# Channel products of the Fourier branch folded into the last attention pair, pair order, norm products and output weights moved, in an eight-core encoder layer

## The reference

```python
proj = x @ w_in                       # q, k, v (24 heads of 64), u_f (512), gate_a, gate_f (1024 each)
# three groups of 8 heads: windows 128, 512, 2048 with dilations 1, 4, 16; relative-position bias
attn = sum over groups of softmax(lse)[g] * out[g]         # 512 wide
y_attn = attn @ w_attn_out
f = real(fft2(u_f as (positions, 4 groups of 128 channels), ortho))
y_four = f @ w_fourier_out
mix = (sigmoid(gate_a) * y_attn + sigmoid(gate_f) * y_four) @ w_out
h = layer_norm(alpha * x + mix)
out = layer_norm(alpha * h + square(relu(h @ w_up + b_up)) @ w_down + b_down)
```

## Time and profile before

| | |
|---|---|
| median of 3 runs | 2229.06 us (2223.16 to 2231.4) |
| the profiled execution | 2229.99 us, span 2228.5 us on core 4 |
| spans of the 8 cores | 2204.2 to 2228.5 us |
| mean granted clock of TensorE, core 4 | 0.981 |
| PE busy | 2072.9 us (93%) |
| DVE busy | 1087.7 us (49%) |
| ACT busy | 694.3 us (31%) |
| POOL busy | 178.6 us (8%) |

### The profile page before, as it was taken

How to read it: one execution, slowest core, us unless ns; L and a number is a source line. 1 busy time by engine, 2 the same in 40 slices (tenths; PEclk the granted TensorE clock), 3 DMA queues, 4 the chain that set the end, 5 groups by cost and what they waited for, 6 DMA issues and landing times.

```text
span 2228.5 us, 39457 instructions; the slowest of 8 cores (2204.2 to 2228.5 us)
## 1 busy us (share of the span) xinstructions
PE 2072.9 (93%) x10660; PEld 991.5 (44%) x10866; DVE 1087.7 (49%) x1704; ACT 694.3 (31%) x1182; POOL 178.6 (8%) x234
## 2 busy tenths in 40 slices
PE   5999778899989999999999999989999999999997
PEld 2454334444444444444444544443444444444443
DVE  1235567534574555555232366675337535554543
ACT  1446445222232221313124455532221413122130
POOL 1000000000000110202020000000000002020011
PEclk9999999999999999999999999989999999999999
DMA  9428456554143453548731123154113345454352
GB/s 143 68 39 107 88 86 126 121 156 86 38 171 133 154 192 132 195 134 216 190 96 34 25 46 60 27 125 161 29 20 123 134 136 188 151 179 171 122 200 95
DMA packets 61468, 261.56 MB, mean 117 GB/s; under 512 B 8050, under 2 KB 19314, under 8 KB 41084
## 3 DMA queue, kind: packets, MB, share of 16 engines
q1 hardware_dynamic: 34084, 194.54, 25.8%
q0 software_dynamic: 27168, 64.49, 18.6%
HBM read 306.43 MB, written 35.91 MB: 154 GB/s over the span
## 4 chain that ended last, share of the span: by engine, by line
PE 81%; DMA 9%; DVE 5%; issue 3%; ACT 1%; POOL 0%; DVEq 0%; POOLq 0%; ACTq 0%; SPq 0%
PE bank L329 76%; PE bank L327 4%; DMA pool<-wup_s 3%; DMA pool<-rden_s 2%; DMA pool<-xt 1%; DMA pool<-wdn_s 1%; ACT pool L318 1%; DMA pool<-dft 1%; PE bank L984 1%; DVE pool L1158 1%; DVE pool L704 0%; DVE pool L922 0%; DVE pool L709 0%; DVE pool L655 0%; DMA rden_s<-pool 0%
## 5 line engine op out<-in xcount | busy, mean ns | idle before, releaser
L329 PE MATMUL bank<-pool 128*128 128x512 bf16 (+2 forms) x8686 | 1957.5, 379 | 76.4 <-DMA pool<-xt 22.6
L329 PEld LDWEIGHTS bank<-pool 128*128 128x128 bf16 x8892 | 870.2, 100 | 1053.4 <-issue 142.5
L318 ACT ACTIVATE pool<-bank 128x512 bf16<-128x512 f32 (+7 forms) x290 | 166.6, 580 | 398.4 <-PE bank L329 193.8
L1098 DVE TENSOR_SCALAR pool<-bank,pool 128x512 f32<-128x512 f32 x256 | 187.8, 748 | 148.6 <-PE bank L329 130.2
L1102 ACT ACTIVATE pool<-pool 128x512 bf16<-128x512 f32 x256 | 160.4, 628 | 287.7 <-DVE pool L1098 204.2
L327 PE MATMUL bank<-pool 64*128 64x256 bf16 (+8 forms) x1718 | 176.4, 247 | 57.7 <-DVE pool L655 44.1
L655 DVE TENSOR_TENSOR pool<-pool 128x448 bf16<-128x448 bf16 (+1 forms) x320 | 128.7, 407 | 159.7 <-ACT pool L645 154.9
L645 ACT ACTIVATE pool<-bank 128x448 bf16<-128x448 f32 (+1 forms) x320 | 171.0, 569 | 49.8 <-PE bank L327 46.9
L327 PEld LDWEIGHTS bank<-pool 128*65 128x65 bf16 (+2 forms) x1718 | 109.0, 105 | 153.9 <-issue 96.0
L1039 ACT ACTIVATE pool<-bank 128x512 bf16<-128x512 f32 x128 | 76.2, 597 | 260.6 <-PE bank L329 254.8
L1047 DVE TENSOR_TENSOR pool<-bank,pool 128x512 f32<-128x512 f32 x64 | 44.3, 692 | 171.9 <-PE bank L329 164.3
(11 more groups left out here) (45 smaller groups left out, 568.0 us busy)
## 6 DMA issues: line engine op xcount, KB each, us to landing
pool<-wup_s SPq DMA_DIRECT2D x64, 1024.0 KB, 6.0
pool<-wdn_s SPq DMA_DIRECT2D x64, 1024.0 KB, 5.5
pool<-x SPq DMA_DIRECT2D x32, 512.0 KB, 4.5
out<-pool SPq DMA_DIRECT2D x32, 512.0 KB, 6.9
pool<-wqk POOLq DMA_DIRECT2D x24, 512.0 KB, 7.0
wup_s<-wup POOLq DMA_DIRECT2D x8, 1024.0 KB, 15.6
pool<-rden_s SPq DMA_DIRECT2D x8, 1024.0 KB, 12.4
wdn_s<-wdn POOLq DMA_DIRECT2D x8, 1024.0 KB, 11.2
```

The source lines that it names most:

```text
L318: return kb.op("act", lambda e: e.activation(out=out, in_=in_, func=AF.Copy), reads, writes)
L329: return kb.op("pe", lambda e: e.matmul(out, lhsT, rhs, start=start, stop=stop), reads, writes)
L1098: kb.op("dve", (lambda bk, rb, fc: lambda e: e.tensor_scalar(out=rr[:, rb, :], in0=bk[:, :], scalar1=pvec[:, BUP + fc:BUP + fc + 1], scala ...
```

## The change

Six things, by the code:

- The last three pairs run in the order g = 2, 1, 0, so that pair 9 is 16-dilated and pair 11 undilated. Whether a merge copies or adds now depends on the place (`fresh`, the first of the three).
- The reciprocal (`norm_rec`) is issued at the last but one item of the first pair of a pp, and the norm products at the last four items of the second, cut by position block. `attnT` gets seven resources, the last pp's one for each position block.
- The folds of chunks 0 and 1 stand in pair 10, the channel products (`ab_steps`, 136 matmuls, 9 steps an item) in pair 11, the next folds behind them, with two buffers instead of three.
- The values `V` are three tiles, each freed after its last pair; the two halves of the cosine and sine tables get one buffer each there (`dft0`, `dft1`), loaded at pairs 10 and 11. `wao` is loaded at pair 11, the first gate weights right after it, `wfo` once the last broadcast of reciprocals has landed.
- In the Fourier stage the midpoint comes after the first cosine products, `reft` and `nyq` are tracked by halves, the rows of `nyq` are moved after each half, the last norm products come after the first half's combinations, and the first gate blocks run ahead of the products with `wao` and `wfo`.
- Several tiles have other places; the layer norm's vector `vg1` and the first residual rows are loaded before the gates instead of in their last chunk.

The core of the diff (`dense_for(11)` runs `ab_steps`):

```diff
-    pair_order = [4 * g + pp for pp in range(4) for g in range(3)]
+    pairs = [(pp, g) for pp in range(4) for g in ((0, 1, 2) if pp < 3 else (2, 1, 0))]
+    pair_order = [4 * g + pp for pp, g in pairs]
...
             def norm_mul(pp_, part=None):
                 acc, acc_r = accs[pp_ % 2]
                 attnT, attnT_r = attn_t
-                for e2 in range(2):
-                    for tq in ((0, 1), (2, 3))[part % 2] if part is not None and part // 2 == e2 else (
-                            range(4) if part is None else ()):
+                for tq in range(4) if part is None else (part,):
+                    for e2 in range(2):
                         cs = slice(tq * 512, (tq + 1) * 512)
                         kb.op("dve", (lambda cs, e2: lambda e: e.tensor_tensor(
                             out=attnT[64 * e2:64 * e2 + 64, pp_, cs], in0=acc[0:64, e2, cs], in1=rbc[:, e2, cs],
-                            op=ALU.mult))(cs, e2), [acc_r[e2]] + rbc_r, [attnT_r[pp_]])
+                            op=ALU.mult))(cs, e2), [acc_r[e2]] + rbc_r, [attnT_r[pp_ if pp_ < 3 else 3 + tq]])
...
+            def ab_steps():
+                for c in range(8):
+                    for eo, n0, n1 in ((0, 0, 260), (1, 260, 516)):
+                        if len(bank_free) < 2:
+                            run_late()
+                        bk, br = next_bank()
+                        for dc in range(8):
+                            mm(bk[:, 0:n1 - n0], xeo[:, c % 2, eo, dc, :], wfc[:, dc, n0:n1], dc == 0, dc == 7,
+                               [xeo_r[c % 2], wfc_r[dc]], [br])
+                            if dc == 7:
+                                def ev(bk=bk, br=br, c=c, eo=eo, n0=n0, n1=n1):
+                                    evac_copy(AB[:, c, n0:n1], bk[:, 0:n1 - n0], [br], [AB_r[2 * c + eo]], eng="act")
+                                    bfree(br)
+                                    if eo == 1 and c + 2 < 8:
+                                        fold(c + 2)
+                                late.append(ev)
+                            yield
...
-            dftb, dftb_r = place(s, "dftb", BF16, [2, 8, 512], 182144, nres=2)
-            dft_ring = Ring(4, 2, lambda k, b: dma("sp", dftb[:, b], dft_d[k // 2, k % 2], writes=[dftb_r[b]]))
-
-            NDENSE = [192, 192] + [80 if s == 0 else 64] * 2 + [64] * 7 + [0]
+            fx = {}
+
+            NDENSE = [192, 192] + [80 if s == 0 else 64] * 2 + [64] * 7 + [144]
+            AB, AB_r = place(s, "AB", BF16, [8, 516], 182144, nres=16)
+            xeo, xeo_r = place(s, "xeo", BF16, [2, 2, 8, 128], 190400, nres=2)
...
+                                    if fresh:
+                                        kb.op("dve", lambda e: e.tensor_copy(out=av, in_=src), [obr], [acc_r[e2]])
+                                    else:
                                         kb.op("dve", lambda e: e.tensor_tensor(out=av, in0=src, in1=av, op=ALU.add),
...
+                    if pair_i == 10:
+                        mem.free("V2")
+                        fx["dft0"] = place(s, "dft0", BF16, [2, 8, 512], 116224, nres=2)
                     if pair_i == 11:
-                        dft_ring.need(0)
+                        mem.free("V1", "acc0", "wqk")
+                        fx["dft1"] = place(s, "dft1", BF16, [2, 8, 512], 99584, nres=2)
+                        c1024, c1024_r = place(s, "c1024", BF16, [S], 149248, parts=1)
+                        a1024, a1024_r = place(s, "a1024", BF16, [260], 153344, parts=1)
+                        fx["a1024"] = (a1024, a1024_r)
+                        dma("sp", c1024, c1024_d, writes=c1024_r)
+                        wao, wao_r = place(s, "wao", BF16, [4, D], 65536)
+                        dma("pool", wao, wao_d, writes=wao_r)
+                    if pair_i >= 10:
+                        tb, tb_r = fx["dft%d" % (pair_i - 10)]
+                        for k in range(2):
+                            dma("sp", tb[:, k], dft_d[pair_i - 10, k], writes=[tb_r[k]])
...
-                        if pending_norm is not None and g == 1:
-                            if ii == 1:
-                                norm_rec()
-                            if 9 <= ii < 13:
-                                norm_mul(pending_norm, ii - 9)
-                            if ii == 12:
+                        if pending_norm is not None and pair_i % 3 == 0 and ii == len(items) - 2:
+                            norm_rec()
+                        if pending_norm is not None and pair_i % 3 == 1 and ii >= len(items) - 4:
+                            norm_mul(pending_norm, ii - len(items) + 4)
+                            if ii == len(items) - 1:
                                 pending_norm = None
+                        if pair_i == 10 and ii in (8, 10):
+                            fold((ii - 8) // 2)
...
+            load_wg(0, 0)
...
+                    dma("pool", wfo, wfo_d, after=[norm_rec()], writes=wfo_r)
...
+                for m in range(2):
+                    for cs in ((slice(0, 512), slice(S - 510, S)) if kt == 0 else (slice(512, S - 510),)):
+                        dma("sp", reft[0:128:64, 2 + m, cs], nyq[2 * m:2 * m + 2, cs], reads=nyq_r if kt else [nyq_r[0]],
+                            writes=[reft_r[4 + 2 * m + kt]])
+                if kt == 0:
+                    norm_mul(pending_norm)
+                    mem.free("acc1", "rbc", "rd")
...
+                    if dc > 0 or tq not in (1, 2):
+                        gates(tq)
+                    if dc == 0 and tq == 0:
+                        gates(1)
                     bka, bra = next_bank()
                     for hp in range(4):
                         mm(bka[:, :], wao[:, hp, dc * 128:(dc + 1) * 128], attnT[:, hp, cs], hp == 0, hp == 3,
-                           attnT_r + wao_r, [bra])
...
+                    if dc == 0 and tq == 1:
+                        gates(2)
                     bkf, brf = next_bank()
                     for gq in range(4):
                         mm(bkf[:, :], wfo[:, gq, dc * 128:(dc + 1) * 128], reft[:, gq, cs], gq == 0, gq == 3,
-                           reft_r + wfo_r, [brf])
+                           reft_r[0::2] * (tq in (0, 3)) + reft_r[1::2] * (tq > 0) + wfo_r, [brf])
```

More of the change, by code:

```diff
@@ L508, in run_late @@
                 late.clear()
-            pairs = [(pp, g) for pp in range(4) for g in range(3)]
             for tq in range(4):
@@ L590, in dense_for @@
                         yield
+                if k == 11:
+                    for _ in ab_steps():
+                        yield
                 if s == 0 and k in (2, 3):
@@ L845, in run_seq @@
                 if kt == 0:
[L846 to L848 removed]
+                    bkh, brh = next_bank()
+                    for c in range(9):
+                        for m in range(3):
+                            a, z = msl[m]
+                            if c < 8:
+                                mm(bkh[0:z - a, m:m + 1], AB[:, c, a:z], alt[:, 0:1], c == 0 and m == 0, False,
+                                   [AEr[c]] + alt_r, [brh], skip=True)
+                            else:
+                                mm(bkh[0:z - a, m:m + 1], a1024[0:1, a:z], c1024[0:1, H:H + 1], False, True,
+                                   a1024_r + c1024_r, [brh], skip=True)
+                    evac_copy(nyq[:, H:H + 1], bkh[0:4, 2:3], [brh], [nyq_r[1]], eng="act")
+                    for ch in range(4):
+                        evac_copy(reft[:, ch, H:H + 1], bkh[:, ch % 2:ch % 2 + 1], [brh], [reft_r[2 * ch + 1]], eng="act")
+                    bfree(brh)
+                    dma("pool", wfo, wfo_d, after=[norm_rec()], writes=wfo_r)
                 qb = [next_bank() for _ in range(2)]
[L850 removed]
                 for c in range(8):
@@ L1027, in run_seq, with gates @@
                     mem.free("wgA")
-                    vg1, vg1_r = place(s, "vg1", F32, [D], 81920)
-                    xr_ring.need(0)
-                    dma("sp", vg1, vecb_d[:, 0, :], writes=vg1_r)
-                for tq in range(4):
+                    Rs.append(place(s, "R0", F32, [4, D], 135168, nres=4))
+                def gates(tq):
                     cs = slice(tq * 512, (tq + 1) * 512)
```

169 lines of the change are left out of this document (71 added, 98 removed).

## The result

The changed kernel takes 2208.07 us (median; the runs of the kernel before beside it 2230.23). The ratio is 0.9895, 95% interval 0.9851 to 0.9938; measured again, 2211.54 us and 0.9908 (0.9883 to 0.9932). It is faster, by some 20 us, where 2173 was forecast with a range down to 2153 and up to 2197. The sign was right and a little over a third of the gain came.

The account below looks back on a forecast made before the run. TensorE, with 81% of the chain, was taken as the bound, so only its stops or lower clock could be won: 27.1 us at the norm products plus 29.5 from pair 9 to the gates, 56.6 in all, giving 2173 us, range 2153 to 2197.

Parts of the forecast that it names:

- the stop in pair 7 of the first sequence: Wait at the norm products; pair 7 took 33.07 us against 21.04 with TensorE full; its removal was to gain 9.5.
- The 2.2 taken from it: Loss of pair 10 in the kernel before, whose norm products don't wait; basis for 2.5 us per such pair.
- The norm products: Earlier reciprocal, later products: broadcast gets 14 items instead of 8, waits in pairs 4 and 7 go; gain 27.1 us.
- The residue: Loss left in each pair with norm products at its last four items, as VectorE falls behind: 2.5 us taken.
- Pairs 9 to 11: New order with channel products in pair 11: 17.65 us for pair 9, 49.5 for pairs 10 and 11.
- Rival (b): VectorE bounds pair 11 through dearer merges and waits for folds: 9 us a sequence, 2191 us; chance 0.17.
- The Fourier stage: After pair 11: 21.0 us of TensorE work, no waits for tables, plus 2.5 us a sequence for thin margins.
- the last chain: Last denominators' store, reload, reciprocal, broadcast, products and combinations before the first gates: 2.5 us a sequence, between 0 and 8.
- rival (c): The last denominators' reload takes the full 11.2 us, weights and last halves come 6 to 8 late: 2185; chance 0.10.
- (a): Broadcast of reciprocals still late in the first sequence, stretched to 25 us by casts in flight: 2183 to 2186; chance 0.10.
- (d): Small waits in pairs 10 and 11 keep the clock at 0.50 through the Fourier stage: +86 us, 2259; chance 0.03.

Follow-up runs that it names:

- norm_alone: Kernel before with only the new places of reciprocal (last but one item of the pair before) and norm products (last four items): 2229.33 us, 1.0004.
- norm_alone_cm: Kernel before with the new norm places, and the weight casts moved out of pairs 9 to 11 and the first two gate chunks: 2215.94 us, 0.9947.
- cm_prod_next: casts_moved with the norm products of the first two pp put one an item into the following 16-dilated pairs (5 and 8): 2175.78 us, 0.9769.
- casts_moved: Changed kernel with the weight casts moved from pairs 9 to 11 and the first two gate chunks to gate chunks 2 to 7: 2192.62 us, 0.9839.
- combined: cm_prod_next with pair 10's norm products one an item at items 6 to 13 and its folds at items 1 and 3: 2168.24 us, 0.9733.

## Why the prediction was wrong

**What bounds the kernel.** The reading of the rows held: the stops at the norm products were the largest loss of the slowest core. Two limits of it: the stop in pair 7 of the first sequence, priced at 9.5, stood in that execution on cores 0, 4 and 6 alone (no other core waits 2 us there), and the earlier trace rows calls 377.61 the first score of pair 11, where the row shows value products. The 2.2 taken from it is about right all the same: pairs 4 and 7 of the second sequence took 27.1 and 25.7 us, which less 21.04 and their stops of 3.48 and 2.13 leaves 2.6.

**The norm products, the step that failed.** I wrote that the broadcast "has 14 items instead of 8", and let the waits go. For the broadcast that was right: in the profiled execution no core waits for it after. What I left out is the other end of the same move. The reciprocal waits for the reload, and that lost three items of its time in every pp, and in pair 9 more, because a 16-dilated pair of 17.65 us now stands in the place of one of 21.04: from 18.1 us behind the reload's issue (338.13 to 356.27) to 10.9. The sum put this wait at nothing, without a reason. I had the reload's 11.2 us, a median, and the 19.73 us of a DMA beside a cast, and used the first only at the end of pair 11; the trace also had 17.9 us for this very reload. It took 25.3. The reciprocal stands in DVE's queue ahead of the mask products, so its wait became 12.6 us of PE. With the clock behind it pair 9 lost 114.6-9.54-91.5 = 13.6 us against the second sequence. Forecast 27.1 us for this part; the changed kernel got 8.3+6.9 in pairs 4 and 7 of the first sequence (46.3 and 43.8 us with the pair behind them, against 54.6 and 50.7) and 2.3+0.8 in the second, 18.3 in all, of which the 13.6 were lost again. norm_alone shows the whole of it as zero, norm_alone_cm the 8 us that are left without the casts.

**The residue.** I took 2.5 us for each pair with products. In the second sequence of the changed kernel it is 2.2 to 5.1 on the eight cores, against 38.69 for the two pairs: 2.2 where the clock stayed at 1.00, more where it fell, which I priced only for long stops. cm_prod_next shows the size in time: 16 us for four pairs.

**Pairs 9 to 11.** 49.5 us for pairs 10 and 11 was forecast, 51.2 measured in the second sequence of the changed kernel (1431.84 to 1483.02), 50.9 in casts_moved. The merge on contiguous columns takes 0.68 to 0.69 us in the rows of pair 11, against 0.69 taken. Rival (b) did not happen. The gain over the kernel before in the second sequence, 104.7 to 91.5, was 13.2 of the 14.0 forecast. But the folding is only 4 to 5 of that. Another 4.5 are two stops of the kernel before that the changed one doesn't have: 2.2 us for a table and 2.3 for a fold. The table waits of the kernel before, both sequences:

```profile
PE bank L329 <- DMA pool<-dft: 5.7, 2, 3.5
```

In the first sequence they were 3.5 to 6.7 us on every core. The last 4 us or so of the 13.2 no run takes apart.

**The Fourier stage.** 2.5 us a sequence with at most 8 for the last chain. The second sequence had none. In the first PE waited up to 9.5 us for the Fourier rows, and not for the reason of rival (c): the reload took 2.3 us there (400.73 to 403.07), and the rows, which I had put at 2 us, were under way for 15.35 beside a cast (426.13 to 441.48 in the chain). casts_moved, where no core waits 2 us for them, shows it. The midpoint's new place costs up to 3 us of lower clock a sequence, which the sum doesn't have.

**The rivals.** (a) fell, though its cause, a cast in flight, was the right one, at another DMA; for the broadcast itself no run took the cast away. (d) did not happen; the clock fell for short stretches only. The range was too narrow because no case of it had a new wait in the first sequence as long as the old one. casts_moved has neither of the two new waits and is still some 20 us above the forecast. An estimate of that from the rows: up to 2.6 us of residue above the 2.5 in each of four pairs, and in each sequence 1.4 in pairs 10 and 11 and up to 3 behind the midpoint, in sum at most 19. With the products really one pair later cm_prod_next takes 2175.78, close to the 2173. That is in part luck: it gains by taking away residues that the forecast had counted in, and still has the dips that the forecast left out.

**The account.** On the profiled slowest cores the account is +18.3 in the norm pairs, -8.5 in the first stretch from pair 9 to the gates and +13.2 in the second, 23.0 us, where the spans differ by 21.1.

## What to carry to other kernels

When a step is moved earlier, price both ends: what it feeds gets more time, and what feeds it gets less, and if it stands in an in-order queue its new wait belongs to everything behind it. A small DMA that someone waits for should not share its time with bulk copies that nobody waits for yet; here moving the casts was worth 15 us together with the change, and without it some 4, with an interval that reaches to no change. Look up such a DMA at its own place and not by its median: 11.2 us was the median of three reloads, 17.9 the one that mattered. Work that has to go onto a half-loaded engine did best here in the pair whose items last longest (16 us).

## What the runs showed of the hardware

- A reload of 16 KB took 25.3 us beside two DRAM-to-DRAM casts in the changed kernel. At one place in two kernels that differ by the casts alone, it took 17.9 to 21.7 us with them and 3.9 to 5.7 without. The rows of the special columns, waited for up to 9.5 us with a cast beside them, were waited for 2 us or more on no core without it. The casts are on another queue than the small DMAs.
- TensorE busy for 6.00 of 6 us had a granted clock of 0.50 behind 27 one-column matmuls that followed the cosine products (a fall in 14 of 16 stretches), and mostly 1.00 when the same 27 followed the sine products (a fall in 2 of 16). The Trainium skill, "TensorE: Matmul & The Clock Gate", "What's actually happening", says that the gate goes by how busy the engine has been. Read as the busy share of the profile's rows, that doesn't fit: the fall stands in a window of 6.00 of 6 us busy, and the measurement decides.
- Two stops of 1.5 us close together in a pair left the mean clock of two pairs at 1.00 on some cores and brought it to 0.96 or 0.92 on others (casts_moved), for 40.9, 42.3 to 42.6 or 43.6 to 43.9 us of the same work.
- The slowest core of one execution is not that of the next: core 1 of the changed kernel had spans of 2207.4, 2181.5 and 2205.3 us. With the waits for small DMAs gone (combined), the eight lie within 10.9 us.
